# HGRN2 layers of a four-layer trunk: v projected token-major for two heads at once, states and values later in a round

## What is computed

```python
h = rms_norm(x, norm_w[layer])
q, f, inp_v, g = jnp.split(h @ w_in, 4, axis=-1)      # w_in: 1024 x 4096
q = silu(q); k = (1 - lb) * sigmoid(-f); log_f = ...  # f and lb give the decay
# per head, causal, over chunks of tokens:
o = scores @ vc + (qc * exp(b)) @ state
state = exp(b_last)[..., None] * state + (kc * exp(b_last - b)).T @ vc
y = rms_norm(o, o_norm_w) * silu(g)
x = x + y @ w_out
```

## Time and profile before

| | |
|---|---|
| median of 3 runs | 1348.59 us (1348.59 to 1348.66) |
| span of the profiled execution | 1346.8 us |
| instructions | 22178 |
| weight loads (PEld) | 1118.0 us busy, 83% of the span |
| DVE | 923.1 us busy, 69% |
| ACT | 687.2 us busy, 51% |
| POOL | 145.3 us busy, 11% |
| DMA | 113.62 MB, 84 GB/s on average |

### The profile page before, as it was taken

One profiled execution on the slowest core, in us unless ns is written; L12 is line 12 of the kernel. 1 busy time (PEld: TensorE's weight loads), 2 busy tenths in 40 slices (PEclk: granted clock), 3 DMA queues, 4 the chain that ended last, 5 costly groups with the idle time before them and its releaser, 6 DMA issues.

```text
span 1346.8 us, 22178 instructions
## 1 busy us (share of the span) xinstructions
PE 1339.1 (99%) x8759; PEld 1118.0 (83%) x8759; DVE 923.1 (69%) x1659; ACT 687.2 (51%) x1226; POOL 145.3 (11%) x224
## 2 busy tenths in 40 slices
PE   9999999999999999999999999999999999999999
PEld 8888888888888888888888887788888888888887
DVE  7867778564767576666676676865657577777782
ACT  6445555353655565656565656553434335454550
POOL 2422333000000000000000000000000022332220
DMA  6322233423222222222223131332333322232221
GB/s 194 95 80 79 64 94 95 118 79 91 66 79 79 79 79 79 79 79 79 79 68 90 48 92 50 105 93 71 94 94 94 110 76 83 63 93 76 84 64 63
DMA packets 211688, 113.62 MB, mean 84 GB/s; under 512 B 3743, under 2 KB 209889, under 8 KB 211586
## 3 DMA queue, kind: packets, MB, share of 16 engines
q1 hardware_dynamic: 211202, 112.02, 28.9%
q0 software_dynamic: 384, 0.20, 0.1%
HBM read 110.10 MB, written 2.10 MB: 83 GB/s over the span
## 4 chain that ended last, share of the span: by engine, by line
PE 96%; DVE 2%; ACT 1%; issue 1%; DMA 0%; SPq 0%; ACTq 0%; DVEq 0%
PE ps L647 39%; PE ps L662 38%; PE scores L662 4%; PE ps L1088 2%; PE ps L1072 2%; PE ps L1028 2%; PE ps L881 1%; PE scores L1056 1%; PE ps L1056 1%; PE scores L852 1%; PE ps L676 1%; PE ps L883 1%; PE scores L870 1%; PE scores L819 1%; PE ps L892 1%
## 5 line engine op out<-in xcount | busy, mean ns | idle before, releaser
L647 PE MATMUL ps<-op_hi,w_hi 128*128 128x512 f32 (+1 forms) x800 | 311.7, 390 | 0.0
L647 PE MATMUL ps<-op_lo,w_hi 128*128 128x512 f32 (+1 forms) x800 | 305.4, 382 | 0.0
L647 PE MATMUL ps<-op_hi,w_lo 128*128 128x512 f32 (+1 forms) x800 | 304.5, 381 | 0.0
L662 PE MATMUL ps<-w_hi,op_hi 128*128 128x512 f32 (+1 forms) x728 | 294.0, 404 | 1.6 <-DVE op_lo L1844 1.6
L662 PE MATMUL ps<-w_lo,op_hi 128*128 128x512 f32 (+1 forms) x728 | 282.6, 388 | 0.0
L662 PE MATMUL ps<-w_hi,op_lo 128*128 128x512 f32 (+1 forms) x728 | 282.2, 388 | 0.0
L1786 DVE TENSOR_TENSOR w_lo<-raw,w_hi 128x1024 fp32r<-128x1024 f32 x200 | 245.1, 1251 | 12.4 <-ACT w_hi L1274 10.9
L1274 ACT ACTIVATE w_hi<-raw 128x1024 fp32r<-128x1024 f32 x200 | 203.0, 1052 | 26.8 <-PE ps L662 11.2
L647 PEld LDWEIGHTS ps<-op_lo,w_hi 128*128 128x128 f32 x800 | 150.4, 188 | 29.9
L647 PEld LDWEIGHTS ps<-op_hi,w_hi 128*128 128x128 f32 x800 | 150.5, 188 | 27.4 <-DVE op_lo L1829 0.2
L647 PEld LDWEIGHTS ps<-op_hi,w_lo 128*128 128x128 f32 x800 | 150.7, 188 | 27.0
(11 more groups left out here) (228 smaller groups left out, 1944.9 us busy)
## 6 DMA issues: line engine op xcount, KB each, us to landing
raw<-in_b_w_in SPq DMA_DIRECT2D x80, 512.0 KB, 3.9
raw<-in_a_w_in SPq DMA_DIRECT2D x64, 512.0 KB, 4.2
raw<-in_c_w_in SPq DMA_DIRECT2D x24, 512.0 KB, 4.1
raw<-in_a_w_out SPq DMA_DIRECT2D x16, 512.0 KB, 4.3
raw<-in_b_w_out SPq DMA_DIRECT2D x8, 512.0 KB, 4.0
raw<-in_c_w_out SPq DMA_DIRECT2D x8, 512.0 KB, 4.9
xt<-in_x SPq DMA_DIRECT2D x4, 512.0 KB, 6.2
y<-in_norm_w SPq DMA_DIRECT2D x3, 512.0 KB, 4.7
```

Of the source, the lines that this page charges most:

```text
L647: last = nc.tensor.matmul(bank, a, b, start=(k == 0 and p == 0), stop=(k == KT - 1 and p == 2))
L662: last = nc.tensor.matmul(bank, a, b, start=(k == 0 and p == 0), stop=(k == KT - 1 and p == 2))
```

## The change

v is no longer projected head by head in feature-major form. In each round two of the four token tiles are projected for two heads at once: v_step issues token_step with 256 columns, a slice of two neighbouring ring slots. An even round i does tiles 0 and 1 of heads i and i + 1, the odd round after it tiles 2 and 3 of the same two. ACT copies the bank straight into a_v01 or a_v23, where states and values read it. turn_v, v_out and a_vt go. The v chunk of head i + 1 is loaded and split in round i, so round 0 has five chunks and round 7 three. states (with turn_o) moves from after step 20 to after step 26, values from after step 25 to after step 31. Round 7 has no step 31, so its values stand in the tail, behind gate_bank(3, 4, 5, 6, 7). On ACT the squares and the root of a head come one round later, and so do o_squares and o_norm on DVE. Also on DVE, carry and into_y move behind the queries of the first two levels and the weight splits of the next round.

```diff
+def a_order(i):
+
+    of_v = ((2, 0), (2, 1)) if i == 0 else ((2, i + 1),) if i + 1 < HEADS else ()
+    return ((1, i), (0, i)) + of_v + ((3, i),)
...
+def a_v_slot(head):
+
+    return (HALF + 2, HALF)[head // 2 % 2] + head % 2
...
+        def v_half(of):
+
+            return a_v23 if of % 2 else a_v01[:, of // 2 % 2 * 2:of // 2 % 2 * 2 + 2]
```

On PE:

```diff
-                    def turn_v():
...
+                    def v_step(k):
+
+                        slot = a_v_slot(i // 2 * 2)
+                        for half in (2 * k, 2 * k + 1):
+                            t, of = divmod(half, KT)
+                            last = token_step(acc[0][:, t * 2 * P:(t + 1) * 2 * P], slice(slot, slot + 2), of,
+                                              i % 2 * 2 + t)
+                        return last
...
                     def states():
                         pe.wait_ge(kT_done, h + 1)
-                        pe.wait_ge(vT_done, h + 1)
+                        pe.wait_ge(v_act, h // 2 * 2 + 2)
...
                     if mix and not proj:
-                        turn_v()
                         gate_bank(3, 4, 5, 6, 7)
+                        values(h - 1)
                         scores()
...
-                        steps[17] = [turn_v, turn_k]
-                        steps[20] = [turn_o, states] if end else [states]
-                        steps[25] = [values]
+                        steps[17] = [turn_k]
+                        steps[26] = [turn_o, states] if end else [states]
+                        if not last_proj:
+                            steps[31] = [lambda: values(h)]
                         steps[6] = [scores]
                     if last_proj:
                         for k in range(3):
-                            steps.setdefault(24 + k, []).append(lambda k=k: gate_bank(k))
+                            steps.setdefault(24 + k, []).insert(0, lambda k=k: gate_bank(k))
```

On ACT:

```diff
                     if mix and not proj:
-                        v_out()
                         freed_y(0, 1, 2)
                         gate_sigmoid()
-                        freed_y(3, 4, 5)
+                        freed_y(3, 4)
+                        square(h - 1)
+                        freed_y(5)
                         root(h - 1)
...
-                        split_chunks(IN0[n], per, j, par, (2, 3), ring)
+                        for part, of in a_order(i)[2:]:
+                            split_part(i, part, of)
+                        if end:
+                            square(h - 1)
...
                         if mix:
-                            v_out()
                             k_out()
+                        if end:
+                            root(h - 1)
                         if not last_proj:
-                            split_chunks(IN0[n], per, j if par == 0 else j + 1, 1 - par, (0, 1), a_ring)
+                            for part in (1, 0):
+                                split_part(i + 1, part, i + 1)
```

On DVE:

```diff
                     if proj:
-                        split_lo_chunk(IN0[n], len(A_PARTS), j, par, 2, ring)
+                        for part, of in a_order(i)[2:-1]:
+                            split_part(i, part, of)
+                    if proj and end:
+                        o_squares(h - 1)
...
+                    if end:
+                        o_norm(h - 1)
+                    move_queries(0, a_q[:, par], head, par, 0)
+                    far_queries(0)
+                    farthest_queries(0)
+                    if not last_proj:
+                        for part in (1, 0):
+                            split_part(i + 1, part, i + 1)
+                    next_queries(0)
+                    far_queries(1)
+                    farthest_queries(1)
                     if mix:
                         carry()
                     if end:
                         into_y()
-                    if not last_proj:
-                        for c in (0, 1):
-                            split_lo_chunk(IN0[n], len(A_PARTS), j if par == 0 else j + 1, 1 - par, c, a_ring)
-                    move_queries(0, a_q[:, par], head, par, 0)
-                    far_queries(0)
-                    farthest_queries(0)
-                    if mix and not last_proj:
-                        o_squares(h)
-                    next_queries(0)
-                    if mix and not last_proj:
-                        o_norm(h)
...
+                    next_queries(1)
+                    far_queries(2)
+                    farthest_queries(2)
```

More of the change, by code:

```diff
@@ L86, with a_number, a_ring @@
 ACC0 = [sum(ACC_OF[:n]) for n in range(4)]
-def a_ring(par, c):
-    return c // 2 * HALF + c % 2
-def a_last_ring(par, c):
-    return SLOTS - 1 if c == 3 else a_ring(par, c)
+def a_order(i):
+    of_v = ((2, 0), (2, 1)) if i == 0 else ((2, i + 1),) if i + 1 < HEADS else ()
+    return ((1, i), (0, i)) + of_v + ((3, i),)
+def a_number(i, part, head):
+    return sum(len(a_order(n)) for n in range(i)) + a_order(i).index((part, head))
+def a_v_slot(head):
+    return (HALF + 2, HALF)[head // 2 % 2] + head % 2
+def a_ring(part, head):
+    return (1, 0, a_v_slot(head), SLOTS - 1 if head == HEADS - 1 else 2)[part]
 def b_ring(par, c):
@@ L518, in load_first, with load_a @@
                 for c in chunks:
-                    w, col = ((a_w_in[n // 3], A_PARTS[c] * D) if n % 3 == 0 else
+                    w, col = ((a_w_in[n // 3], a_order(0)[c][0] * D + a_order(0)[c][1] * P) if n % 3 == 0 else
                               (b_w_in[0], B_PARTS[c] * D) if n == 1 else (c_w_in[0], D + c * P))
                     load((IN0[n] + c) % RAW, columns(w, col), IN0[n] + c)
+            def load_a(n):
+                for i in range(HEADS):
+                    for c, (part, head) in enumerate(a_order(i)):
+                        if i == 0 and c < (RAW if n else 2):
+                            continue
+                        at = IN0[n] + a_number(i, part, head)
+                        load(at % RAW, columns(a_w_in[n // 3], part * D + head * P), at)
             def load_layer(n, w, parts):
@@ L987, in body @@
                             steps[3].append(lambda k=k: wide(n, k, (2, 3)))
-                    for ks in range(len(A_PARTS) * KT):
+                    for ks in range(A_CHUNKS * KT):
                         c, k = divmod(ks, KT)
+                        part = (1, 0, 2, 3)[c]
                         if proj and static(i) and i == 0 and c < 2:
-                            last = feature_step(acc[c][:, 256:S], a_ring(par, c), k, slice(256, S))
+                            last = feature_step(acc[c][:, 256:S], a_ring(part, i), k, slice(256, S))
                             if k == KT - 1:
@@ L1374, in layer_a, with split_part @@
             def layer_a(n, idx):
-                H0, A0, per = HEADS * idx, ACC0[n], len(A_PARTS)
+                H0, A0 = HEADS * idx, ACC0[n]
+                def split_part(i, part, head):
+                    at = IN0[n] + a_number(i, part, head)
+                    split_hi(at % RAW, 16 * (at // RAW + 1), a_ring(part, head), at)
                 def body(j, par, proj, mix, end):
```

87 lines of the change are left out of this document (36 added, 51 removed).

## The result

The changed kernel takes 1359.03 us (median, 1358.84 to 1359.53), the kernel before 1348.59 us; the ratio is 1.0077 with a 95% interval of 1.0064 to 1.0090. It is slower by 0.8%, 10.4 us, where 4.1 were predicted. The profiled execution has a span of 1357.1 us, 10.3 more than the one before, so the two traces can be set against each other term by term.

The account below looks back on a forecast made before the run. PE's hole-free matmul stream was taken as the bound. Per layer: round 0 +0.32, six rounds -0.90, round 7 and tail +2.3, so +1.75; two layers +3.5, first start +0.6: +4.1, 1352.7 us, range 1346.3 to 1355.0.

Parts of the forecast that it names:

- Part 1: Rounds 1 to 8 of each HGRN2 layer: the four transposes of turn_v go, 0.44 us of PE a round.
- Part 2: v as 48 matmuls of 256 columns at 0.120 us: +0.32 us a round, less 0.03 for returns from fp32 matmuls.
- rival B: v matmuls run at 0.1133 us each instead of 0.120: 1347.6 us, no change; chance 0.12.
- Part 5: Round 0 of the first layer: ACT's third weight split delays the v matmuls, a hole of about 0.6 us, once.
- part 4: Round 7 and tail: next_queries(1) waits for values, delaying splits and the first output matmul; +2.3 us a layer, hole 3.0 us.
- rival D: Steady rounds: root holds up o_norm, the 1.2 us before values don't hold, holes in 12 rounds; 1357.5 us, chance 0.08.
- Part 3: Steady rounds' new order: DVE's carry ends over 1 us before PE reaches values, so it costs nothing.
- both tails 1 us worse: Upper end of the predicted range: main case A with each tail 1 us worse, 1355.0 us.

Follow-up runs that it names:

- experiment 5: Kernel before without the four transposes of v a round and ACT's copy of them, so v stays untransposed: 1343.76 us, ratio 0.9963.
- experiment 4: Kernel before, v still feature-major, but made as 48 matmuls of 256 columns instead of 24 of 512: 1352.92 us, ratio 1.0030.
- Experiment 10: Changed kernel with one wait added, so GpSimd's last two key moves of the last head start after the first two splits of y: 1355.12 us, ratio 1.0046.
- Experiment 3: Changed kernel with 13 useless 128-column matmuls filling PE's hole between the tail's scores and first wide output matmul: 1355.23 us, ratio 1.0045.
- Experiment 11: Changed kernel with carry one place sooner on DVE, ahead of the second pair of far queries: 1358.98 us, ratio 1.0077.
- experiments 1: Changed kernel with DVE's two splits of output weights moved ahead of next_queries(1), which waits for values: 1348.82 us, ratio to the kernel before 1.0003.
- experiment 2: Changed kernel with 24 useless 128-column matmuls between the tail's scores and the first wide output matmul: 1359.21 us, ratio 1.0078.
- experiment 6: Changed kernel with the tail's values ahead of gate_bank(7), three matmuls sooner: 1356.27 us, ratio 1.0053.
- experiment 7: Changed kernel with output-weight splits ahead of next_queries(1), plus root right behind square and o_norm right behind o_squares: 1348.96 us, ratio 1.0001.

## Why the prediction went wrong

**Right.** Part 1: the transposes gave 0.43 a round (experiment 5, predicted 0.44). Part 2: the v form ran at 0.119 us and costs 0.26 with its returns (experiment 4; predicted 0.32 less 0.03); rival B is out. Steady rounds that don't wait are 0.16 shorter (predicted 0.15). Part 5: the hole in round 0 is 0.6 us as predicted; from the transposes of vec_rows to the scores of round 1 it is 22.82 us instead of 21.83, +0.99, for 0.6 + 0.32 predicted. Layer 4's round 0 has its +0.32. In part 4 the mechanism and the moments of PE and of DVE's release were right to a tenth.

**Part 4's size: 3.2 a tail instead of 2.3.** The term that failed is "Two splits 2.27 ... the first split_y 0.68". They were read off a place of the kernel before where GpSimd was idle (its key moves started at 230.76, behind them). In the new order they lie beside its key moves and take 2.70 and 1.10. Experiment 10 moves GpSimd away and gets 0.85 a tail back. 1.7 us of the 6.3 missing.

**The half clock: 3.0 us, left out of the sum.** The prediction had the 3.0 us hole, named the rule that an idle array falls back, said that no row showed what that does, and then gave it only as a part of D's chance. Experiment 3 prices it by filling the hole: 1.46 and 1.58 us, against the changed kernel's first profile, whose granted clock of 0.997 is at the upper end of its four runs (0.995 to 0.997). A hole two and a half times as long as any in the trace (3.0 us to 1.2) should have had a price from both sides in the range: nothing at one end, and at the other a few us of matmuls at 0.43 instead of 0.23 us. This was the larger mistake, of method rather than of size.

**Part 3's cover: 0.2 us instead of 1.2.** By the row of the steady round DVE needs 8.6 us from the end of pair_products (L1999 at 136.73 + 0.43) to the end of carry, where the working had 7.8. The excess is nearly all in the two splits, 2.93 us from start to start (139.54 to 142.47) for 2.3 taken. GpSimd's next_keys runs at the same time, two of its instructions taking 1.50 and 1.32 us (L639 at 139.96, L643 at 141.54) where the same two take 0.48 and 0.41 a little later; that it is the cause is carried over from the tail, where experiment 10 shows it. PE was at values 8.8 us after that point (forecast 9.0). That "nothing" as the cost held in 19 of the 24 steady rounds of the two profiles, with 0.1 us to spare, was luck. The rest was used up in two rounds of one profile and three of the other, 0.5 us each: rival D's place, at a fifth to a quarter of its price. D's reason isn't theirs: it had o_norm held up by root, and o_norm waits 0.2 us for root in both kinds of round, as the working had it. The long rounds differ in DVE's work beside GpSimd, 8.88 us for 8.36, mostly in the queries. Experiment 11 gives the room back by moving carry. It is open what decides in which rounds it happens: the five profiles of variants that leave the steady rounds as they are (experiments 1, 2, 3, 6 and 10) have no round above 27.10 us, and that DVE time is 8.34 to 8.37 in them, while both profiles of the changed kernel itself have long ones, with 8.85 to 8.88. It is also open why experiment 11 gained nothing in time.

**Lead-in.** 0.44 of the first line of the table lies ahead of anything that the change touches: the transposes of vec_rows start at 21.51 us before, at 21.95 in the changed kernel, at 21.66 in its second profile. The three profiles in the old order have 20.95 to 21.51, the eleven in the new one 21.05 to 21.98. They overlap, so one pair of profiles can't tell a cost from scatter, and a difference of spans carries up to 0.9 us of it.

Together, against the 4.1 us of the forecast: tails +1.8 (3.25 and 3.19 for 2.3 each), half clock +3.0, long rounds +0.9, lead-in +0.4, gives 10.2 for 10.3 measured. The direction was right, the size wrong by more than the range allowed. The range's upper end was built from "both tails 1 us worse", which the tails' own excess nearly used up, and nothing in it stood for the clock.

## What to carry to other kernels

When an instruction is put behind a wait on an in-order engine, list what is queued behind it and what of that the critical engine needs next; here two weight splits a layer that needed nothing from the wait cost 8.7 us in the tails and behind them, and with them in front of it the time was that of the kernel before. Take durations for the moved work from a stretch where its neighbours are the ones that it will have, and expect that work moved into the gap changes places with other work beside the same neighbour (experiment 7). If a hole opens that is longer than any in the trace, price the clock behind the hole as a term with two ends. A saving ahead of a stretch that another engine bounds (the tail, by DVE) doesn't arrive: the transposes' 0.44 us came through in the steady rounds alone.

## What was not expected of the hardware

- After a hole of 3.2 us the granted clock was at the 1.2 GHz level for a part of the next ten us (means of 0.83 and 0.84), costing 1.4 to 1.6 us. In other profiles a hole of 3.1 us cost 2.9 (experiment 6), one of 3.2 cost 2.5 (experiment 11), and one of 2.35 us cost 1.6 in one layer and nothing in the other (experiment 10). Behind the hole of 1.2 us in the middle of the kernel (at 871.72 after, 865.59 before) the clock was 1.00 in all fourteen profiles.
- Useless matmuls in the hole kept the clock at 1.00. They ran at 0.22 us each for 128 columns in fp32 (experiment 2).
- DVE's weight split (two SBUF inputs, 128x1024) takes 1.13 us from start to start alone and 1.5 to 1.6 beside GpSimd's tensor_tensor; GpSimd's two moves take 2.37 us beside it and 1.64 beside DVE's gate and a shorter split of y.
